# The first MLP's down projection: 14 of its 22 K blocks plain, the last 8 as a chunk of seven half-size products

## The chip, the cores and the metric

The kernel runs on one core of a Trainium2 chip. The metric is the device time of one execution in microseconds (us); lower is better. Inputs and outputs are float32. A product of two float32 matrices is made of three TensorE matmuls on rounded parts: each operand is split into a high part (rounded to fp32r) and a low part (the operand less its high part), and high by high, high by low and low by high are summed.

## The reference

Two blocks of two layers with an MLP each, on a sequence of 512 tokens and a model width of 1024. The change is in the first layer's MLP, whose hidden width is 2816 (22 blocks of 128):

```python
h2 = rms_norm(x, ffn_norm)
u = causal_dwconv(h2 @ w_up, conv_w, conv_b)
a, bval = jnp.split(u, 2, axis=-1)
return x + (jax.nn.silu(a) * bval) @ w_down
```

After it comes a block with dilated window attention (its QKV projection is the next large product), an MLP of width 4096 (MLP2 of layer 0), a differential attention, and a second MLP of width 4096 (MLP2 of layer 1). In these:

```python
def sq_relu_mlp(xn, w_in, w_out):
    h = jax.nn.relu(xn @ w_in)
    return (h * h) @ w_out
```

## The kernel before

Activations are kept transposed: 128 features on the partitions, 512 tokens along the free axis. `x` is 8 such blocks of 128x512. Weights come from HBM in tiles of 128x1024 (512 KB) by SyncE's queue (SP) into the two halves of `stage`. ScalarE (ACT) writes the high part of a tile (`split_hi`, here `down_split_hi`), GpSimd (POOL) the low part (`split_lo`, here `down_split_lo`, in four instructions of 128x256), and a stage half is free for the next load when POOL is done with it (`lo_ready`). VectorE (DVE) reads the finished PSUM banks. Nothing orders the engines but semaphores, and each engine works its own instructions strictly in the order written in its block.

**The up projection of the first MLP** ends with `Q_UP` = 17 rounds of seven half-size products each (84 matmuls of 128x256 a round, L1309, L1310, L1317). Beside it, DVE and ACT do the convolution (L2065, L2924, L2927), the silu (L2071), and POOL forms block f of the gated hidden layer `f1[f]` (`f_made_of`, L760). A block f is needed in two parts: `f_high(f)` on ACT (L2135) and `f_low(f)` on DVE (L3024).

**The down projection** (`for d in range(KD)`, L1342 to L1376) makes the 8 output blocks d one after the other, each over all 22 blocks f: 22 x 3 matmuls of 128x512 into PSUM bank `G[d % 2]` (L1360 high by high, L1362 and L1339 high by low, L1369 low by high). Its 176 weight blocks are packed 8 to a tile, so `N_DOWN1` = 22 tiles and an output block is 2.75 tiles. Output block 0 has its high by low products (`first_by_low`, L1339) put last, since those low parts are made latest. When a block is done DVE adds the bank to `x[:, d]` (L3090) and forms the next layer's low input with `low_x` (L2591), and ACT its high part (L2242) and square (L2243). The bank may be written again for block d + 2 once DVE's addition has counted up `evac`.

**The seven half-size products** (Winograd's form of Strassen's algorithm) are used by MLP2's down projection: a chunk of 8 K blocks by 512 tokens is multiplied with 4 groups ("quads") of 256 output features. One quad is 7 products over 4 pairs of K blocks, 3 matmuls of 128x256 for each pair (`product`, L1735, L1736, L1744), 84 matmuls in place of 2 x 8 x 3 = 48 of 128x512. Its operands are sums of quarters: on the weights' side 8 highs by ACT (`quad_copy`, `quad_high`), 4 sums and 2 lows by DVE (`quad_sum`, `quad_low`), 5 lows by POOL (`quad_lows`); on the activations' side per pair of K blocks the four sums and seven high and low factors (`fc_hi`, `fc_lo`), made by ACT and DVE as the K blocks get ready. The seven results are added to `x` by DVE in quarters (`add_product`, L3512).

Of the kernel before, what the change touches and what calls it, by code (L numbers as in the profile page):

```python
# [16 lines left out]
F32 = mybir.dt.float32  # L17
F32R = mybir.dt.float32r
ALU = mybir.AluOpType
# [37 lines left out]
N_DOWN1 = KD * NF1 // KD  # L57
# [15 lines left out]
EVAC_SKIP = (N_UP1 + N_DOWN1) // 2 - KD // 2 - WO_HALVES  # L73
# [15 lines left out]
Q_LAST = 2 * N_CH * QUADS - 1  # L89
# [27 lines left out]
N_EARLY = 8  # L117
EARLY_AT = 4
POOL_LOWS = []
DVE_LOWS = [f for f in range(NF1) if f not in POOL_LOWS]  # L120
FFH_PREP = FF_PREP = 2 * QUADS
X_LOWS = QUADS + 1
FFH_BEFORE, FF_BEFORE = FFH_PREP + NF1, FF_PREP + len(DVE_LOWS)
# [7 lines left out]
def quad_at(l, n):  # L131

    return QUADS * (N_CH * l + n)


def fc_at(l, n, i):

    return N_FC * l + 2 * KD * n + 4 * i
# [37 lines left out]
def program(nc, x_in, params, consts, buckets, swa_table, weights, pairs, tables, out):  # L176
    with ExitStack() as ctx:
# [77 lines left out]
        f_home = [arena[:, N_IN_ARENA + 4 * c + b] for c in F_FREE for b in range(4)]  # L255
        f1_hi = [(w_hi, w_lo)[f // 2 % 2][:, f // 4].rearrange("p (a k) c -> p a (k c)", a=2)[:, f % 2] for f in range(N_EARLY)]
        f1_hi += f_home[N_EARLY:NF1]
        f1_lo = [arena[:, f] for f in range(N_IN_ARENA)] + f_home[NF1:]

        def down_hi(t):  # L260

            if t == T_DOWN1 + 3:
                return v_split[:, 0].rearrange("p b t f -> p (b t) f")
            if t == T_DOWN1 + 2:
                return bias_slots[:, 0:2].rearrange("p a (c f) -> p (a c) f", f=P)
            a = N_IN_ARENA + 4 * F_FREE[t % 2]
            return arena[:, a:a + 2].rearrange("p a (c f) -> p (a c) f", f=P)

        def down_lo(t):

            if t == T_DOWN1 + 3:
                return v_split[:, 1].rearrange("p b t f -> p (b t) f")
            if t == T_DOWN1 + 2:
                return bias_slots[:, 2:4].rearrange("p a (c f) -> p (a c) f", f=P)
            a = N_IN_ARENA + 4 * F_FREE[t % 2] + 2
            return arena[:, a:a + 2].rearrange("p a (c f) -> p (a c) f", f=P)
# [96 lines left out]
        up_moved, down_done = sem("up_moved"), sem("down_done")  # L373
# [130 lines left out]
        def _(sp):  # L504
# [109 lines left out]
            loads(T_DOWN1, T_QKV[0])  # L614
            sp.wait_ge(tables_saved, 80)
            for l, core in enumerate((dil, dif)):
                T = T_QKV[l]
                if l == 1:
                    loads(T, T + 2)
                    sp.wait_ge(dil.maxed, 8 * PAIRS)  # L620
                for p in range(2):
                    bias_load(core, tables[l], p, p, None)
                loads(T + 2 * l, T + 8)
# [18 lines left out]
        def _(pool):  # L642
# [60 lines left out]

            def mlp2_splits(l):

                for n in range(N_CH):
# [11 lines left out]
                    ends = n == N_CH - 1  # L718
                    for j in range(1, QUADS):
                        quad_lows(q + j, (HI_A11,))  # L720
                        if ends and j > 1:
                            square_sum(4 + 2 * l, 2 * j - 4)
                        quad_lows(q + j, (HI_A12,))
                        if ends and j > 1:
                            square_sum(4 + 2 * l, 2 * j - 3)
                        quad_lows(q + j, (HI_S4, HI_S3, HI_A22))
                square_sum(4 + 2 * l, 4)
                square_sum(4 + 2 * l, 5)
# [33 lines left out]
            def f_low(f):  # L762

                pool.wait_ge(ffh_ready, FFH_PREP + f + 1)
                nc.gpsimd.tensor_tensor(f1_lo[f], f1[f], f1_hi[f].bitcast(F32), ALU.subtract).then_inc(factor_low, 1)

            def down_low(t):

                for k in range(0, KD, KD // 4):
# [4 lines left out]
            def down_split_lo(t):  # L774

                pool.wait_ge(hi_ready, t + 1)
                down_low(t)
# [32 lines left out]
            down_split_lo(T_DOWN1 + 2)  # L810
            for f in POOL_LOWS:
                f_low(f)
            pool.wait_ge(ff_ready, FF_PREP + 20)
            down_split_lo(T_DOWN1 + 3)
            with pool.Fori((T_DOWN1 + 4) // 2, T_QKV[0] // 2) as m:
                for p_ in range(2):
                    pool.wait_ge(hi_ready, 2 * m + p_ + 1)
                    pool.wait_ge(tile_done, 2 * m + p_ - 1)
                    down_low(T_DOWN1 + 4 + p_)
            split_los(T_QKV[0], T_MLP2[0])  # L820
# [47 lines left out]
        def _(pe):  # L868
# [466 lines left out]
            def first_by_low(s_, ks):  # L1335

                for k, f in ks:
                    pe.wait_ge(ff_ready, FF_PREP + f + 1)
                    mm = pe.matmul(G[0][:], down_hi(T_DOWN1 + s_)[:, k], f1_lo[f], start=False, stop=(f == NF1 - 1))  # L1339
                mm.then_inc(hi_free if ks[-1][0] == KD - 1 else down_done, 1)  # L1340

            for d in range(KD):  # L1342
                pieces = []
                for f in range(NF1):
                    s_, k = divmod(d * NF1 + f, KD)
                    if k == 0 or f == 0:
                        pieces.append((s_, []))
                    pieces[-1][1].append((k, f))
                if d < 2:
                    pe.wait_ge(conv_2, 2 * (NF1 - 1))  # L1350
                else:
                    pe.wait_ge(evac[d % 2], T_MLP1 // 2 + WO_HALVES + d // 2)
                for s_, ks in pieces:
                    t = T_DOWN1 + s_
                    ends = ks[-1][0] == KD - 1
                    pe.wait_ge(hi_ready, t + 1)
                    for k, f in ks:
                        if d == 0:
                            pe.wait_ge(ffh_ready, FFH_PREP + f + 1)
                        pe.matmul(G[d % 2][:], down_hi(t)[:, k], f1_hi[f], start=(f == 0), stop=False)  # L1360
                        if d:
                            mm = pe.matmul(G[d % 2][:], down_hi(t)[:, k], f1_lo[f], start=False, stop=False)  # L1362
                    if d and ends:
                        mm.then_inc(hi_free, 1)
                    if d == 0 and s_ == 2:
                        first_by_low(*pieces[0])
                    pe.wait_ge(lo_ready, t + 1)
                    for k, f in ks:
                        mm = pe.matmul(G[d % 2][:], down_lo(t)[:, k], f1_hi[f], start=False, stop=(d > 0 and f == NF1 - 1))  # L1369
                    if ends:  # L1370
                        mm.then_inc(tile_done, 1)
                    elif d and f == NF1 - 1:
                        mm.then_inc(down_done, 1)
                if d == 0:
                    for s_, ks in pieces[1:]:
                        first_by_low(s_, ks)  # L1376
# [7 lines left out]
            def layer_a():  # L1384
# [89 lines left out]
                norm(2)  # L1474
                tile(T // 2, 1, xn_hi, xn_lo)
# [237 lines left out]

            def product(l, n, q, k, quads):

                j, s = q % QUADS, q % 2
                region = R2 if k in (HI_A12, HI_A22) else R5 if k in (HI_S1, HI_S4) else R1[s][:, 0:HS]
                fresh = k in (HI_A11, HI_S1, HI_A12, HI_A22)
                f = FACTORS[k]
                if quads[0] == 0:  # L1720
                    pe.wait_ge(slot_high, UP_HIGHS + N_HIGH * q + k + 2)
                    read = N_PROD * q + {HI_A11: -N_PROD, HI_S1: -2, HI_A12: 0, HI_S2: 1, HI_S4: 2, HI_S3: 4, HI_A22: 3}[k]
                    if q == Q_LAST and k in (HI_S3, HI_A22):
                        read = N_PROD * q + LAST_ADDS["u2" if k == HI_S3 else "p2"]
                    if read > 0:
                        pe.wait_ge(product_added, UP_ADDED + read)
                high = {F_B11: 1, F_T1: 2, F_B21: 3, F_B22: 3, F_T3: 4, F_T2: 4, F_T4: 4}[f]
                for i in quads:
                    w = slot_hi[k][:, i * P:(i + 1) * P]
                    if j == 0 and i == QUADS - 1 and f == F_T2:  # L1730
                        pe.wait_ge(factor_low, X_LOWS + N_CH * l + n + 1)
                    elif j == 0:
                        pe.wait_ge(ffh_ready, FFH_BEFORE + fc_at(l, n, i) + high)
# [2069 lines left out]
```

## Time and profile before

| | us |
|---|---|
| median of 3 runs | 1696.07 |
| lowest and highest | 1695.65, 1696.42 |
| the profiled execution, its own time | 1695.82 |
| its span, first to last instruction | 1693.8 |
| TensorE busy in the span | 1684.6 (99%) |
| VectorE busy | 1128.9 (67%) |
| ScalarE busy | 909.3 (54%) |
| GpSimd busy | 1018.8 (60%) |

The profile is of one execution. A busy time is the union of an engine's instructions, and the duration of a matmul includes its pipelined end, so the pace of matmuls is read from the distance of their starts or from the chain of waits, not from the mean of one. The chain of waits lists what released what, back from the last instruction; a piece that stands in it with `x8` is eight instructions in a row. Stretches below are given in us from the start of the span: the down projection is 422.38 to 542.16, and the last chunk of MLP2 of layer 0 is 1060.72 to 1101.04.

### The profile page before, as it was taken

Reading aid. Unit: us, or ns where it says so; the run is one execution under the profiler, and the core shown is the slowest. Engines: PE = TensorE matmul, PEld = TensorE weight load, DVE = VectorE, ACT = ScalarE, POOL = GpSimd, SP = SyncE. Lnnn points to the kernel's source line nnn. Section 1 sums busy time; section 2 is a strip of 40 time slices with the busy share of each in tenths; the row PEclk is TensorE's granted clock in tenths of the full one; section 3 lists DMA queues with packets and bytes.
Section 4 is the critical chain, followed back from the end, with each engine's and each line's share of the span. In section 5 each row is a group of like instructions: output and inputs, shape, how many; then the busy total and the mean of one; then the engine's idle time right before and its main releaser. Section 6 shows DMA issues by size and latency. Waiting matters only on the chain.

```text
span 1693.8 us, 28396 instructions
## 1 busy us (share of the span) xinstructions
PE 1684.6 (99%) x10031; PEld 1460.3 (86%) x10031; DVE 1128.9 (67%) x2244; ACT 909.3 (54%) x1665; POOL 1018.8 (60%) x1071
## 2 busy tenths in 40 slices
PE   9999999999999999999999999999999999999998
PEld 7778889999888888888989898977777889898988
DVE  6875888887412455667766666777777675757576
ACT  5665658787423444345444444656565553535355
POOL 6543688777554444357575757755554666666666
PEclk9999999999999999999999999999999999999999
DMA  5221333222334322223323233232331343333332
GB/s 194 77 69 63 106 110 125 101 100 88 92 95 143 97 69 85 75 87 112 113 87 112 89 111 96 98 121 84 119 106 50 90 135 100 99 100 100 100 100 75
DMA packets 48555, 168.37 MB, mean 99 GB/s; under 512 B 5216, under 2 KB 6512, under 8 KB 48432
## 3 DMA queue, kind: packets, MB, share of 16 engines
q1 hardware_dynamic: 48144, 166.23, 30.5%
q8 instruction: 73, 1.20, 0.3%
q10 hardware_dynamic: 288, 0.53, 0.1%
q14 instruction: 50, 0.41, 0.1%
HBM read 164.49 MB, written 2.24 MB: 98 GB/s over the span
## 4 chain that ended last, share of the span: by engine, by line
PE 96%; DVE 2%; ACT 1%; POOL 1%; DMA 1%; issue 1%; DVEq 0%; ACTq 0%
PE bank L970 19%; PE bank L889 7%; PE bank L888 7%; PE bank L894 7%; PE bank L1735 6%; PE bank L1744 6%; PE bank L1736 6%; PE bank L1309 3%; PE bank L1317 3%; PE bank L1310 3%; PE bank L988 3%; PE bank L994 3%; PE bank L989 3%; PE bank L1369 2%; PE bank L1360 2%; PE bank L1362 2%
## 5 line engine op out<-in xcount | busy, mean ns | idle before, releaser
L648 POOL TENSOR_TENSOR w_lo<-stage,w_hi 128x256 fp32r<-128x256 f32 x648 | 512.5, 823 | 414.7 <-ACT w_hi L1797 212.8
L1797 ACT ACTIVATE w_hi<-stage 128x1024 fp32r<-128x1024 f32 x162 | 170.6, 1053 | 162.0 <-PE bank L970 49.7
L888 PE MATMUL bank<-xn_hi,w_hi 128*128 128x512 f32 x544 | 211.8, 389 | 0.0
L889 PE MATMUL bank<-xn_lo,w_hi 128*128 128x512 f32 x544 | 211.7, 389 | 0.0
L970 PE MATMUL bank<-xn_hi,w_hi 128*128 128x512 f32 x464 | 188.1, 405 | 0.0
L970 PE MATMUL bank<-xn_lo,w_hi 128*128 128x512 f32 x464 | 181.8, 392 | 0.0
L3512 DVE TENSOR_TENSOR x_space<-x_space,bank 128x256 f32<-128x256 f32 (+1 forms) x217 | 96.7, 454 | 86.9 <-PE bank L1744 85.0
L1744 PE MATMUL bank<-arena 128*128 128x256 f32 x896 | 146.6, 283 | 0.0
L894 PE MATMUL bank<-xn_hi,w_lo 128*128 128x512 f32 x544 | 135.0, 389 | 0.0
L1735 PE MATMUL bank<-arena 128*128 128x256 f32 x512 | 128.8, 283 | 0.0
L1736 PE MATMUL bank<-arena 128*128 128x256 f32 x512 | 128.7, 283 | 0.0
L1744 PEld LDWEIGHTS bank<-arena 128*128 128x128 f32 x896 | 124.8, 192 | 0.0
L970 PE MATMUL bank<-xn_hi,w_lo 128*128 128x512 f32 x464 | 123.5, 398 | 0.0
L894 PEld LDWEIGHTS bank<-xn_hi,w_lo 128*128 128x128 f32 x544 | 102.1, 188 | 21.2
L889 PEld LDWEIGHTS bank<-xn_lo,w_hi 128*128 128x128 f32 x544 | 102.1, 188 | 21.0
L888 PEld LDWEIGHTS bank<-xn_hi,w_hi 128*128 128x128 f32 x544 | 102.2, 188 | 21.0
L3532 DVE TENSOR_TENSOR arena<-tmp,arena 128x256 fp32r<-128x256 f32 (+2 forms) x120 | 107.7, 918 | 3.9 <-ACT arena L2536 2.5
L970 PEld LDWEIGHTS bank<-xn_hi,w_hi 128*128 128x128 f32 x464 | 87.2, 188 | 21.0 <-issue 4.2
L970 PEld LDWEIGHTS bank<-xn_hi,w_lo 128*128 128x128 f32 x464 | 84.7, 188 | 21.5 <-issue 4.7
L970 PEld LDWEIGHTS bank<-xn_lo,w_hi 128*128 128x128 f32 x464 | 87.3, 188 | 16.4
L1735 PEld LDWEIGHTS bank<-arena 128*128 128x128 f32 x512 | 98.3, 192 | 0.1
L1736 PEld LDWEIGHTS bank<-arena 128*128 128x128 f32 x512 | 98.3, 192 | 0.0
(517 smaller groups left out, 4352.3 us busy)
## 6 DMA issues: line engine op xcount, KB each, us to landing
stage<-weights SPq DMA_DIRECT2D x185, 512.0 KB, 3.5
stage<-pairs SPq DMA_DIRECT2D x48, 512.0 KB, 3.6
prob<-pairs SPq DMA_DIRECT2D x32, 512.0 KB, 3.6
bias<-table SPq DMA_DIRECT2D x11, 896.0 KB, 5.9
xn_raw<-pairs SPq DMA_DIRECT2D x16, 512.0 KB, 4.0
out<-y SPq DMA_DIRECT2D x8, 256.0 KB, 2.3
x_space<-x_in SPq DMA_DIRECT2D x3, 512.0 KB, 7.4
bias<-swa_table SPq DMA_DIRECT2D x4, 256.0 KB, 3.7
```

Source lines behind the costliest of these rows:

```text
L648: ins = nc.gpsimd.tensor_tensor(w_lo[:, p_, ks], stage[:, p_, ks], w_hi[:, p_, ks].bitcast(F32), ALU.subtract)
L888: pe.matmul(G[p_][:], w_hi[:, p_, k], hi[:, k], start=(first and k == ks[0]), stop=False)
L889: mm = pe.matmul(G[p_][:], w_hi[:, p_, k], lo[:, k], start=False, stop=False)
L894: mm = pe.matmul(G[p_][:], w_lo[:, p_, k], hi[:, k], start=False, stop=(last and k == ks[-1]))
L970: mm = pe.matmul(G[p_][:], (w_hi if i < 2 * KD else w_lo)[:, p_, k], (xn_lo if i < 2 * KD and i % 2 else xn_hi)[:, k], start=(i == 0), sto ...
L988: pe.matmul(G[dd][:], w, ff_hi[:, k], start=(k == k0), stop=False)
L1735: pe.matmul(region, w, fc_hi[:, i, f], start=(fresh and i == 0), stop=False, skip_group_check=True)
L1736: pe.matmul(region, w, fc_lo[:, i, f], start=False, stop=False, skip_group_check=True)
L1744: mm = pe.matmul(region, w, fc_hi[:, i, f], start=False, stop=(i == QUADS - 1), skip_group_check=True)
L1797: act.activation(w_hi[:, p_], stage[:, p_], ACT.Copy).then_inc(hi_ready, 1)
L3512: dve.tensor_tensor(dst, dst, src, ALU.add).then_inc(product_added, 1)
L3532: dve.tensor_tensor(fc_lo[:, i, a:b + 1].rearrange("p c s -> p (c s)"), src, fc_hi[:, i, a:b + 1].rearrange("p c s -> p (c s)").bitcast(F3 ...
```

## The change

- The 22 blocks of the down projection are split 6 + 8 + 8. The first 16 tiles (`N_DOWN1 = 2 * KD`) are one tile an output block: tiles 0 to 7 hold 6 K blocks each (the rest of the tile is padding, loaded as before), tiles 8 to 15 hold 8. `down_tile(j)` makes 18 or 24 matmuls in the order high by high and high by low in turn, then low by high; each of the 16 ends with an addition to `x` (`add_down`).
- The last 8 K blocks (`f1[14]` to `f1[21]`) are a chunk of seven half-size products, made by the functions of MLP2, which are taken out of `fast` and `mlp2` (`factor_half`, `first_sums`, `first_highs`, `chunk_highs`, `chunk_lows`, `chunk_adds`, `fast_down`). Their factors are made while tiles 8 to 15 are multiplied, without the relu and square that MLP2 has there. The first chunk's first two additions stand behind all factor work in place of inside it.
- `N_EARLY` (blocks whose high and low parts are made during the up projection) goes from 8 to 6. The parts of blocks 6 to 13 go to other homes, and each waits for the end of the up projection (`product_done`, `N_PROD * Q_UP`).
- The first QKV tiles are loaded when the chunk's last quad has left `stage`; the biases of the attention are loaded after the chunk's quads; the norm's two matmuls go from between the first two QKV tiles to inside the second.

```diff
-N_DOWN1 = KD * NF1 // KD
+NF_PLAIN = 14
+N_DOWN1 = 2 * KD
-N_EARLY = 8
+N_EARLY = 6
 ...
 SyncE
-            loads(T_DOWN1, T_QKV[0])
+            loads(T_DOWN1, T_DOWN1 + KD + 4)
+            sp.wait_ge(tile_done, T_DOWN1 + KD)
+            for r in range(2):
+                quad_load(0, r)
+            loads(T_DOWN1 + KD + 4, T_QKV[0])
+            for r in range(2):
+                sp.wait_ge(lo_ready, T_QKV[0] - 1 + r)
+                quad_load(1, r)
+            for j in range(2, QUADS):
+                for r in range(2):
+                    quad_load(j, r)
             sp.wait_ge(tables_saved, 80)
+            sp.wait_ge(tile_done, T_QKV[0])
+            for p in range(2):
+                bias_load(dil, tables[0], p, p, None)
+            sp.wait_ge(slot_low, UP_LOWS + 5 * QUADS)
             for l, core in enumerate((dil, dif)):
                 T = T_QKV[l]
+                loads(T, T + 2)
 ...
 GpSimd
-                for k in range(0, KD, KD // 4):
+                for k in range(0, KD if t >= T_DOWN1 + KD else N_EARLY, KD // 4):
 ...
+                if t >= T_DOWN1 + 2:
+                    pool.wait_ge(tile_done, t - 1)
 ...
 TensorE
+            def down_tile(j):
+
+                t, d = T_DOWN1 + j, j % KD
+                fs = list(range(N_EARLY) if j < KD else range(N_EARLY, NF_PLAIN))
+                if j < 2:
                     pe.wait_ge(conv_2, 2 * (NF1 - 1))
                 else:
+                    pe.wait_ge(evac[d % 2], T_MLP1 // 2 + WO_HALVES + j // 2)
+                pe.wait_ge(hi_ready, t + 1)
 ...
+            for j in range(N_DOWN1):
+                down_tile(j)
+            fast_down(-1, N_CH - 1)
 ...
                 tile(T // 2, 0, xn_hi, xn_lo, ready=(xn_ready, KD * 2, KD))
-                norm(2)
-                tile(T // 2, 1, xn_hi, xn_lo)
+                tile(T // 2, 1, xn_hi, xn_lo, inside=2)
 ...
 ScalarE
-                    act.wait_ge(product_done, N_PROD * (Q_UP - 1) + f // 4 + 1)
+                    act.wait_ge(product_done, N_PROD * Q_UP)
                 act.activation(f1_hi[f], f1[f], ACT.Copy).then_inc(ffh_ready, 1)
 ...
             silu(NF1 - 1)
-            f_high(14)
-            f_high(15)
+            for f in range(N_EARLY, NF_PLAIN - 2):
+                f_high(f)
             down_split_hi(T_DOWN1 + 2)
-            for f in range(16, NF1):
+            for f in range(NF_PLAIN - 2, NF_PLAIN):
                 f_high(f)
-            down_split_hi(T_DOWN1 + 3)
             load_exp_and_ln()
 ...
+            for t in range(T_DOWN1 + 3, T_DOWN1 + KD + 2):
+                down_split_hi(t)
+            act.wait_ge(f_made, NF1)
+            act.wait_ge(tile_done, T_DOWN1 + KD)
+            act.wait_ge(ff_ready, FF_BEFORE)
+            for e in range(KD):
+                factor_half(-1, N_CH - 1, e, f1[NF_PLAIN + e])
+                if e < KD - 2:
+                    down_split_hi(T_DOWN1 + KD + e + 2)
+                first_highs(0, e)
+            chunk_highs(-1, N_CH - 1)
+            for p_ in range(2):
+                split_hi(T_QKV[0] // 2, p_)
+            split_fast(-1, 0, 3)
 ...
 VectorE
             conv(NF1 - 1, 1)
-            for f in DVE_LOWS:
-                if f > 10:
-                    f_low(f)
+            for f in range(N_EARLY, NF_PLAIN):
+                f_low(f)
 ...
+            def add_down(j):
+
+                dve.wait_ge(tile_done, T_DOWN1 + j + 1)
+                dve.tensor_tensor(x[:, j % KD], x[:, j % KD], G[j % 2][:], ALU.add).then_inc(evac[j % 2], 1)
+
+            for j in range(KD):
+                add_down(j)
             dve.wait_ge(f_made, NF1)
-            dve.memset(acc, 0.0).then_inc(acc_zero, 1)
 ...
+            for e in range(KD):
+                i, p_ = e // 2, e % 2
+                if p_ == 0:
+                    dve.wait_ge(ff_ready, FF_BEFORE + fc_at(-1, N_CH - 1, i))
+                add_down(KD + e)
+                factor_half(-1, N_CH - 1, e, f1[NF_PLAIN + 2 * i], f1[NF_PLAIN + 2 * i + 1])
+                first_sums(0, e)
+            add_product(0, HI_A11)
+            add_product(0, HI_S1)
+            chunk_adds(-1, N_CH - 1)
```

How the change moves instructions shows best at three places. First VectorE where the up projection ends, before (L3024 is `f_low`, L2924 and L2927 the convolution, L3090 the first addition to `x`):

```order
L3009 TENSOR_TENSOR bank<-rstd,bank 128x256 [waits product_done,up_moved]
L3024 TENSOR_TENSOR arena<-arena_raw,arena 128x512 [waits ffh_ready]
L2924 SCALAR_TENSOR_TENSOR tmp<-bank,par,tmp 128x511 [waits conv_0]
L2927 SCALAR_TENSOR_TENSOR tmp<-bank,par,tmp 128x510 [waits conv_1]
L3016 TENSOR_TENSOR bank<-xn_raw,bank 128x256 [waits conv_2,up_moved]
L3017 TENSOR_TENSOR bank<-xn_raw 128x256
L3024 TENSOR_TENSOR arena<-arena_raw,arena 128x512 [waits ffh_ready] x2
L2924 SCALAR_TENSOR_TENSOR tmp<-bank,par,tmp 128x511 [waits conv_0]
L2927 SCALAR_TENSOR_TENSOR tmp<-bank,par,tmp 128x510 [waits conv_1]
L3024 TENSOR_TENSOR arena<-arena_raw,arena 128x512 [waits ffh_ready] x5
L3024 TENSOR_TENSOR arena<-xn_raw,arena 128x512 [waits product_done,ffh_ready] x6
L3090 TENSOR_TENSOR x_space<-x_space,bank 128x512 [waits down_done,acc_zero]
```

The same place on VectorE with the change (L2935 and L2938 are the convolution, L3035 `f_low`, L3242 `add_down`; the x8 and the single one are the additions of tiles 0 to 8):

```order
L2935 SCALAR_TENSOR_TENSOR tmp<-bank,par,tmp 128x511 [waits conv_0]
L2938 SCALAR_TENSOR_TENSOR tmp<-bank,par,tmp 128x510 [waits conv_1]
L3027 TENSOR_TENSOR bank<-xn_raw,bank 128x256 [waits conv_2,up_moved]
L3028 TENSOR_TENSOR bank<-xn_raw 128x256
L3035 TENSOR_TENSOR xn_hi<-arena_raw,bias_slots 128x512 [waits product_done,ffh_ready] x6
L3035 TENSOR_TENSOR xn_lo<-arena_raw,bias_slots 128x512 [waits product_done,ffh_ready]
L3035 TENSOR_TENSOR xn_lo<-arena_raw,rstd_slot 128x512 [waits product_done,ffh_ready]
L3242 TENSOR_TENSOR x_space<-x_space,bank 128x512 [waits tile_done] x8
```

Before, 14 `f_low` stood ahead of the first addition, three of them ahead of the last convolution; now 8 stand there, all behind it.

TensorE at the end of tile 1 and the start of tile 2 with the change (L1366 and L1369 are the high by high and high by low matmuls of `down_tile`, L1373 the low by high ones):

```order
L1373 MATMUL bank<-w_hi,arena 128x512 [waits lo_ready]
L1373 MATMUL bank<-w_hi,arena 128x512
L1373 MATMUL bank<-w_lo,arena 128x512 x2
L1373 MATMUL bank<-w_hi,arena 128x512 x2
L1366 MATMUL bank<-w_hi,arena 128x512 [waits hi_ready,evac0]
L1369 MATMUL bank<-arena 128x512
```

The wait on `evac0`, for the bank of the output block two before, now stands 36 matmuls after the start of the down projection; before it stood 132 matmuls after it.

VectorE where the chunk begins, with the change (L3165 to L3180 are `factor_half` of the last K block, L3134 is `add_product`):

```order
L3242 TENSOR_TENSOR x_space<-x_space,bank 128x512 [waits tile_done]
L3165 TENSOR_TENSOR tmp<-xn_raw 128x256
L3168 TENSOR_TENSOR tmp<-xn_raw,tmp 128x256
L3170 TENSOR_TENSOR tmp<-xn_raw,tmp 128x256 [waits u_ready]
L3154 TENSOR_TENSOR arena<-xn_raw,arena 128x512 [waits ffh_ready]
L3175 TENSOR_TENSOR arena<-tmp,arena 128x256 [waits factor_made]
L3180 TENSOR_TENSOR arena<-tmp,arena 128x2x256 [waits ffh_ready]
L3134 TENSOR_TENSOR x_space<-x_space,bank 128x256 [waits product_done] x2
```

In MLP2 the two L3134 stand after the first L3165 and after L3175; here both stand last.

## Rows read from the trace of the kernel before

**Rows 1.** The page: busy time by engine, and the chain of waits by engine.

```profile
PE 1684.6 (99%) x10031; PEld 1460.3 (86%) x10031; DVE 1128.9 (67%) x2244; ACT 909.3 (54%) x1665; POOL 1018.8 (60%) x1071
...
PE 96%; DVE 2%; ACT 1%; POOL 1%; DMA 1%; issue 1%; DVEq 0%; ACTq 0%
```

**Rows 2.** Waits of TensorE in the whole span: total us, times, longest.

```profile
PE bank L1154 <- DVE arena L2644: 1.5, 1, 1.5
```

**Rows 3.** Busy times of three stretches: length, PE, PEld, DVE, ACT, POOL, clock, DMA.

```profile
422.38:542.16 119.78, 119.78 (x530) 99.05 (x529) 29.88 (x40) 39.06 (x49) 64.77 (x87) 1.00 0.35 111
1060.72:1101.04 40.32, 40.32 (x338) 40.32 (x337) 31.15 (x61) 25.31 (x44) 29.98 (x24) 1.00 0.27 87
1017.21:1060.72 43.51, 43.51 (x194) 36.01 (x194) 29.62 (x40) 21.94 (x35) 29.98 (x33) 1.00 0.34 109
```

**Rows 4.** The chain of waits around 422 and 542: start, us, what.

```profile
421.90 0.48 PE bank L1317 x4
422.38 1.84 PE bank L1360 x8
...
542.16 0.23 PE bank L888
```

**Rows 5.** VectorE in order of time, 419 to 438: start, us, instruction, idle before.

```profile
419.95 1.25 DVE L3024 TENSOR_TENSOR arena<-arena_raw,arena 128x512 fp32r<-128x512 f32 x1
...
423.51 1.28 DVE L3024 TENSOR_TENSOR arena<-arena_raw,arena 128x512 fp32r<-128x512 f32 x2
...
425.49 0.75 DVE L2927 SCALAR_TENSOR_TENSOR tmp<-bank,par,tmp 128x510 f32<-128x510 f32 x1
426.16 5.83 DVE L3024 TENSOR_TENSOR arena<-arena_raw,arena 128x512 fp32r<-128x512 f32 x5
431.91 4.78 DVE L3024 TENSOR_TENSOR arena<-xn_raw,arena 128x512 fp32r<-128x512 f32 x6
...
437.55 0.69 DVE L3090 TENSOR_TENSOR x_space<-x_space,bank 128x512 f32<-128x512 f32 x1 [0.33 <-PE bank L1339]
```

**Rows 6.** ScalarE in order of time, 424 to 433.

```profile
424.83 1.14 ACT L2135 ACTIVATE arena<-arena_raw 128x512 fp32r<-128x512 f32 x2
425.88 1.05 ACT L2144 ACTIVATE bias_slots<-stage 128x1024 fp32r<-128x1024 f32 x1
426.83 3.22 ACT L2135 ACTIVATE arena<-xn_raw 128x512 fp32r<-128x512 f32 x6
...
431.01 1.28 ACT L1837 ACT_TABLE_LOAD   x1
```

**Rows 7.** GpSimd in order of time, 426 to 439.

```profile
426.39 1.61 POOL L760 TENSOR_TENSOR xn_raw<-tmp 128x512 f32<-128x512 f32 x1 [3.19 <-DVE tmp L2927]
427.95 4.62 POOL L771 TENSOR_TENSOR bias_slots<-stage,bias_slots 128x256 fp32r<-128x256 f32 x4
```

**Rows 8.** VectorE and ScalarE in MLP2's fourth factor step, 1039 to 1047.

```profile
1039.78 0.68 DVE L3542 SCALAR_TENSOR_TENSOR tmp<-bank,rstd 128x512 f32<-128x512 f32 x1
...
1041.13 0.62 ACT L2519 ACTIVATE tmp<-tmp 128x512 f32<-128x512 f32 x1
...
1044.12 0.85 ACT L2536 ACTIVATE arena<-tmp 128x768 fp32r<-128x768 f32 x1 [1.70 <-DVE tmp L3557]
...
1045.35 1.05 ACT L1797 ACTIVATE w_hi<-stage 128x1024 fp32r<-128x1024 f32 x1
```

**Rows 9.** VectorE in the same chunk's last factor step, 1061 to 1066.

```profile
1061.26 0.68 DVE L3542 SCALAR_TENSOR_TENSOR tmp<-bank,rstd 128x512 f32<-128x512 f32 x1
1062.64 0.42 DVE L3552 TENSOR_TENSOR tmp<-tmp 128x256 f32<-128x256 f32 x1 [0.70 <-ACT tmp L2519]
...
1065.37 0.68 DVE L3566 TENSOR_TENSOR arena<-tmp,arena 128x512 fp32r<-128x512 f32 x1
```

**Rows 10.** From that chunk into QKV of layer 1: ScalarE, then the chain.

```profile
1099.56 1.06 ACT L1797 ACTIVATE w_hi<-stage 128x1024 fp32r<-128x1024 f32 x1 [0.22 <-DMA stage<-weights]
...
1101.04 0.23 PE bank L888
```

**Rows 11.** The span's first matmuls: duration ns min/median/max, first and last start.

```profile
L1154 PE MATMUL bank<-arena x9: 537/628/792, 1.5 to 5.0; 128*128 128x512 f32 x9
```

More of the change, by code:

```diff
@@ L702, in square_sum, with chunk_lows @@
                 nc.gpsimd.tensor_tensor(acc, acc, tmp[:, d % 2], ALU.add).then_inc(acc_done, 1)
+            def chunk_lows(l, n):
+                q, ends = quad_at(l, n), n == N_CH - 1
+                for j in range(1, QUADS):
+                    quad_lows(q + j, (HI_A11,))
+                    if ends and j > 1:
+                        square_sum(4 + 2 * l, 2 * j - 4)
+                    quad_lows(q + j, (HI_A12,))
+                    if ends and j > 1:
+                        square_sum(4 + 2 * l, 2 * j - 3)
+                    quad_lows(q + j, (HI_S4, HI_S3, HI_A22))
+                if ends:
+                    square_sum(4 + 2 * l, 4)
+                    square_sum(4 + 2 * l, 5)
             def mlp2_splits(l):
@@ L717, in mlp2_splits @@
                     quad_lows(q, (HI_S3, HI_A22))
[L718 to L728, printed above, removed]
+                    chunk_lows(l, n)
                 if l == 0:
@@ new lines, in fast_down @@
+            def fast_down(l, n):
+                every, most, last = list(range(QUADS)), list(range(QUADS - 1)), [QUADS - 1]
+                for j in range(QUADS):
+                    q = quad_at(l, n) + j
+                    if q == Q_LAST:
+                        for k in LAST_ORDER[:-1]:
+                            product(l, n, q, k, every)
+                        last_means(0)
+                        product(l, n, q, HI_A22, every)
+                        last_means(1)
+                        return
+                    product(l, n, q, HI_A11, every)
+                    product(l, n, q, HI_S1, every)
+                    if j == 0:
+                        product(l, n, q, HI_A12, most)
+                        product(l, n, q, HI_S2, most)
+                        product(l, n, q, HI_A12, last)
+                        product(l, n, q, HI_S2, last)
+                    else:
+                        product(l, n, q, HI_A12, every)
+                        product(l, n, q, HI_S2, every)
+                    product(l, n, q, HI_S4, every)
+                    product(l, n, q, HI_S3, every)
+                    product(l, n, q, HI_A22, every)
@@ L3069, in _ @@
                 c_01(q)
-                if not more:
-                    f_low(N_EARLY)
-                elif EARLY_AT <= q < EARLY_AT + N_EARLY:
+                if EARLY_AT <= q < EARLY_AT + N_EARLY:
                     f_low(q - EARLY_AT)
@@ L3613, in fast @@
-                if ends and l == 0:
-                    for k in range(2):
-                        low_fast(l, QUADS - 1, k)
-                        last_square(4 + 2 * l, KD - 2 + k)
+                    factor_half(l, n, e, tmp[:, 0], tmp[:, 1], quad_at(l, n))
+                    first_sums(quad_at(l, n), e)
+                chunk_adds(l, n)
             def mlp2(l):
```

653 lines of the change are left out of this document (295 added, 358 removed).

## The prediction

> **What bounds the kernel now.** I read the page's busy times and chain first [rows 1]: TensorE is busy 99% of the span and holds 96% of the chain, so a saved matmul is saved time, and time that TensorE waits is lost in full. Then TensorE's waits [rows 2]: the longest in the whole span is 1.5 us, at its very start. Then the stretches [rows 3]: in the down projection and in a chunk of MLP2, TensorE is busy for the whole stretch at granted clock 1.00, while no other engine is above 77% of it. The chain at both ends of the down projection [rows 4] shows that TensorE goes from the last up product straight to L1360 at 422.38, and at 542.16 straight to the first QKV matmul. So nothing waits here before; the question is the number of matmuls, and whether the helpers still keep ahead.
>
> **What the matmuls are worth.** The down projection has 528 matmuls of 128x512; eight of them stand for 1.84 us in the chain [rows 4], and 119.78 / 528 = 0.2269 us each [rows 3]. A chunk of MLP2 has 336 matmuls of 128x256 in 40.32 us, 0.12 us each [rows 3]. Eight plain tiles of 24 matmuls took 43.51 us there [rows 3]. The change keeps 336 plain matmuls (14 x 8 x 3) and turns 192 into one chunk: 40.32 in place of 43.51, a gain of **3.2 us**. In columns the saving is one eighth (43.51 / 8 = 5.4 us); since a matmul of half the columns takes more than half the time, 2.2 us of it do not come.
>
> **The first additions, the dearest term.** Tiles 0 to 7 are now 18 matmuls, 4.08 us, each an output block of its own. Tile 2 needs bank `G[0]`, thus VectorE's addition of tile 0 (wait on `evac0`). It is due at 422.38 + 36 x 0.2267 = **430.54**. Before, block 2 came after 132 matmuls, 22 us later than that, and the addition at 437.55 [rows 5] was in good time. In VectorE's queue all eight `f_low(6..13)` stand ahead of it, and they can start only after the last convolution, which ended at 426.24 [rows 5]. The three `f_low` that stood ahead of that convolution are gone; as the convolution also waits for ScalarE I let it end only 0.3 us earlier, 425.95 (an estimate; at most it is 1.28 earlier, the length of two of them).
> One `f_low` took 0.64 us when GpSimd was idle (two in 1.28) and 1.17 us beside GpSimd (five in 5.83, while GpSimd was at work from 426.39 to 432.57) [rows 5, 7]. ScalarE makes six highs from 424.83 at 0.54 each (six in 3.22), then the high part of tile 2 (1.05), so at about 429.1, then the last two highs, ready at 430.1 [rows 6]. GpSimd works on `f1[21]` for 1.6 us from about 426.1, is idle until tile 2's high is there at 429.1, then makes that tile's low part (three instructions now, at 4.62 / 4 each: 3.5 us) and at once tile 3's [rows 7]. So VectorE does 0.2 + 1.4 lows until 427.7, 2.2 until 429.1, and the last 4.2 at 1.17, until about 433.95; the addition takes 0.69 [rows 5]: 434.65. TensorE waits **4.1 us** before tile 2. Bounds: if only ScalarE's last high held VectorE up, 430.1 + 0.64 + 0.69 = 431.4, a wait of 0.9; if all eight took 1.17, 425.95 + 9.4 + 0.7 = 436.0, a wait of 5.5. I take the middle because the rows of this very place show both prices. Behind this addition the one of tile 1 follows within 0.7 us, and no later tile finds its bank full: additions of 0.69 every 4.08 us.
>
> **The weights of tiles 2 to 9.** In 4.08 us ScalarE spends 1.05 [rows 6] and GpSimd three instructions of up to 1.16 us (3.5) [rows 7]. 0, as both are under the tile's time; the padding's load I take as free: a tile is loaded every 4.08 us where it was every 5.44, and DMA was busy 35% of the stretch [rows 3]. The exponential table load (1.28) [rows 6] is moved ahead of tile 3's high, due 438.8: hidden.
>
> **The factors, beside tiles 8 to 15.** ScalarE now has the high part of tile e + 2 behind step e's factors, and these wait for VectorE's addition of tile e. Odd steps are the long ones. In MLP2's, from the start of VectorE's bank read (1039.78) to the end of ScalarE's last factor copy (1044.97) went 5.2 us, of which 1.3 belong to the square that is left out here: 3.9, plus the tile's high 1.05 [rows 8], 4.9 us. A tile is 5.44. VectorE began 0.8 us late in that step, being busy with the quad sums (tile 3's end is 1017.21 + 4 x 5.44 = 1038.97) [rows 3, 8]; with that it is 5.7, 0.3 late, less what the missing square of the step before gives. I take **0.2 us** for all steps. Bounds: 0; and, if the steps were as slow as MLP2's with its square, 1.6 us in each of two steps, 3.2.
>
> **Start and end of the chunk.** TensorE reaches the fourth product, which needs the first product added, after 33 x 0.12 = 3.96 us. VectorE's additions stand behind all factor work now. In MLP2 the last step took from 1061.26 to 1066.05, 4.8 us [rows 9]; without the wait for the square (0.7) and the two additions (0.7), and with the first one at its end (0.4), 3.8: just in time. I take **0.1**, bounds 0 and 1.0 (three of the instructions slowed by GpSimd as above). Into QKV the order is that of MLP2's last chunk, where the second tile's high ended at 1100.62 and TensorE went on at 1101.04 without a gap [rows 10]: 0, with 1 us as the upper bound for the loads now issued that late. The two matmuls of the norm are only moved.
>
> **Sum.** -3.2 + 4.1 + 0.2 + 0.1 = +1.2 us on the profiled execution's 1695.82 gives 1697.0; the median of the runs lies 0.25 above that execution, so **1697.3**. That is +0.07%: within 0.2% (3.4 us, about what a measurement of this kernel can tell from no change). A saving of matmuls that is given back in one new wait.
>
> **Rivals.**
> - *The wait is short.* If VectorE's lows follow ScalarE's highs closely, the wait is the 0.9 us above, or even none, and with the other terms (0.3) the change is worth 2.0 us: 1694.1; with no wait anywhere 3.2: 1692.9. For it: an `f_low` at 0.64 would do eight in 5.1. Against: GpSimd is at work beside them for most of the time in exactly this place [rows 5, 7]. Chance 0.14.
> - *The wait lets TensorE's clock fall.* The only slow matmuls of the trace are the nine after the wait at the start: their starts are 0.44 us apart (8 distances in 3.5 us) [rows 11], twice the 0.227 of the same shape later, which is what 1.2 in place of 2.4 GHz would do. If the 4 us gap did it too, nine such matmuls more would cost 1.9 us: 1699.2; with the longest wait 1700.6. For it: no gap like it exists in the trace [rows 2], so nothing shows that the clock survives one; against: the matmuls around it are dense on both sides. The Trainium skill (TensorE: Matmul & The Clock Gate, Part 1) says that the array's clock is halved after an idle window and restored by sustained work; by that rule an idle gap like this one could bring it about. This is the page that speaks against the change; no row here shows it after the start. Chance 0.15.
> - *The weights come late (the slower side).* If ScalarE's new order (factors first, then the tile's high) misses the 5.44 us in two steps by MLP2's full price, TensorE waits 3.2 us there and not 0.2: 1700.3. It decides once an odd step takes over 5.44 from the end of its tile to the end of the next-but-one's high, and the whole change is slower by over 0.2% once all waits pass 6.6 us. For it: my own count has it 0.3 us from the edge [rows 8]. Against: the square is gone. Chance 0.13.
> The forecast itself keeps 0.58.
>
> **How the numbers follow.** The likeliest case gives 1697.3. The range starts at 1693.0, the case without the wait, and ends at 1700.5, where the third rival and most of the second lie. Faster by over 0.2% (under 1692.7) needs every wait to be hidden and something more: 0.04. Slower by over 0.2% (over 1699.5): the third rival, the second with a wait over 4.1, and the longest waits of the forecast: 0.20. The rest, 0.76, is no change.
>
> **What would show it.** In the profile after, 336 matmuls of `down_tile` at 0.227 and 336 of `product` at 0.12 right behind them; TensorE waiting some 4 us for VectorE's first `x` addition at 430.5, the largest wait in the list; VectorE's eight `f_low` in a row of about 8 us right ahead of it; TensorE from 422.38 to the first QKV matmul about 121 us long in place of 119.78. The clock rival would show as matmul starts 0.44 apart after the gap; the third as waits on ScalarE's tile highs before tiles 13 and 15. Wrong I am if TensorE has no wait before tile 2, or one over 5.5 us, or if it waits after the chunk.

## The result, and the profile after

| | before | after |
|---|---|---|
| median of the runs | 1696.13 us (20 runs) | 1699.38 us (20 runs) |
| lowest to highest | 1695.65 to 1696.63 | 1698.70 to 1700.69 |
| profiled execution: time, span | 1695.82, 1693.8 | 1699.65, 1697.8 |
| mean granted clock of TensorE | 0.999 | 0.998 |

The changed kernel takes 3.25 us more, a ratio of 1.002 with a 95% interval of 1.0014 to 1.0026. That is 2.1 us above the forecast of 1697.3, and 1.1 us inside its upper end. The runs of after are also spread over 2.0 us, those of before over 1.0. Both facts turn out to have one main cause.

The page of after, busy time by engine and the chain of waits by engine; they answer to [rows 1]:

```profile
PE 1683.7 (99%) x10175; PEld 1465.6 (86%) x10175; DVE 1172.5 (69%) x2323; ACT 924.5 (54%) x1700; POOL 1032.5 (61%) x1065
...
PE 93%; DVE 2%; POOL 2%; issue 1%; ACT 1%; DMA 1%; DVEq 0%; SPq 0%; ACTq 0%; POOLq 0%
```

TensorE is busy 0.9 us less than before with 144 instructions more: the matmuls were saved, but not all of their time. Its share of the chain fell from 96% to 93%. TensorE's waits in the whole span (line, releaser: us in total, times, longest), which answer to [rows 2]:

```profile
PE bank L1366 <- DVE x_space L3242: 4.1, 1, 4.1
PE bank L1173 <- DVE arena L2655: 1.5, 1, 1.5
...
PE bank L969 <- DVE arena L2794: 0.4, 1, 0.4
```

L1366 is the first matmul of a plain down tile and L3242 VectorE's addition of a tile to `x`. This is the forecast wait, before tile 2 and of the forecast size. L969 is the norm's matmul in QKV, and new. The stretches of after (length, PE, PEld, DVE, ACT, POOL, granted clock, DMA share, GB/s), which answer to [rows 3]:

```profile
422.58:434.89 12.31, 8.19 (x36) 6.42 (x36) 11.01 (x15) 9.14 (x14) 7.08 (x7) 1.00 0.24 64
434.89:438.56 3.67, 3.67 (x9) 2.96 (x10) 0.54 (x1) 0.00 (x0) 0.62 (x1) 0.54 0.68 208
438.56:504.23 65.67, 65.67 (x290) 54.19 (x290) 30.20 (x46) 23.89 (x35) 37.91 (x49) 1.00 0.34 107
504.23:544.60 40.37, 40.37 (x335) 40.23 (x334) 30.54 (x59) 22.24 (x39) 29.13 (x22) 1.00 0.38 135
```

Tiles 0 and 1 and the wait are the first row. The last row holds nearly all of the chunk, but begins half a microsecond before it; from its own first matmul (504.69) to QKV's first (545.11) the chunk takes 40.42 us, so MLP2's 40.32 again. The second row is what the forecast did not contain: right behind the wait the granted clock is 0.54. In the chain, in order of time (start, us, what), the same place reads:

```profile
434.24 0.61 DVE x_space L3242
434.85 0.04 issue
434.89 0.79 PE bank L1366
435.68 0.43 PE bank L1369
436.11 0.43 PE bank L1366
436.54 0.43 PE bank L1369
...
438.24 0.32 PE bank L1369
438.56 0.23 PE bank L1366
```

Eight matmuls of 128x512 follow each other at 0.43 us (the first is 0.79, with its own latency, and the eighth 0.32), and from 438.56 on at 0.23. That is 1.2 GHz and then 2.4 GHz. At 0.227 each the eight would have taken 1.8 us of these 3.67, so 1.9 us more were lost: about 0.3 to the first matmul's latency after any wait (it takes 0.50 even at full clock, see the filled gap below) and 1.6 to the clock. The ledger of this execution, whose span is 4.0 us longer: matmuls -3.2, wait +4.1, clock and restart +1.9, the down projection's start +0.2 (422.58 for 422.38), the later tiles and the chunk +0.1 together, and +0.9 us at the start of QKV, where the chain reads:

```profile
539.40 5.58 DMA stage<-weights
...
545.00 1.06 ACT w_hi L1798
...
551.71 1.16 DVE arena L2794
552.87 0.04 issue
552.91 0.50 PE bank L969
```

QKV's first two weight tiles landed late (the DMA piece is the second one's), and what stands behind their high parts in ScalarE's queue reached the norm's matmul 0.4 us late; the low products of the first tile were a little late too.

The cause of the wait is VectorE's queue (start, us, instruction, instructions), answering to [rows 5]:

```profile
425.43 0.75 DVE L2938 SCALAR_TENSOR_TENSOR tmp<-bank,par,tmp 128x510 f32<-128x510 f32 x1
426.10 5.87 DVE L3035 TENSOR_TENSOR xn_hi<-arena_raw,bias_slots 128x512 fp32r<-128x512 f32 x6
431.89 1.22 DVE L3035 TENSOR_TENSOR xn_lo<-arena_raw,bias_slots 128x512 fp32r<-128x512 f32 x1
433.03 1.20 DVE L3035 TENSOR_TENSOR xn_lo<-arena_raw,rstd_slot 128x512 fp32r<-128x512 f32 x1
434.16 1.27 DVE L3242 TENSOR_TENSOR x_space<-x_space,bank 128x512 f32<-128x512 f32 x2
```

L3035 is `f_low`. Eight of them take from 426.10 to 434.2, and the two additions stand behind. GpSimd in the same stretch, answering to [rows 7]:

```profile
426.33 1.61 POOL L779 TENSOR_TENSOR xn_raw<-tmp 128x512 f32<-128x512 f32 x1 [4.78 <-DVE tmp L2938]
429.28 6.22 POOL L785 TENSOR_TENSOR arena<-stage,arena 128x256 fp32r<-128x256 f32 x6 [1.34 <-ACT arena L2145]
```

### The profile page after: what moved, and what is told of

The parts are those of the page before. It is cut to its first block, busy times and chain, and to the rows that moved or that the text cites. A ratio compares the mean times of both kernels' runs of the same rounds, so it can differ in the third digit from the quotient of the medians.

```text
span 1697.8 us, 28831 instructions
## 1 busy us (share of the span) xinstructions
PE 1683.7 (99%) x10175; PEld 1465.6 (86%) x10175; DVE 1172.5 (69%) x2323; ACT 924.5 (54%) x1700; POOL 1032.5 (61%) x1065
## 4 chain that ended last, share of the span: by engine, by line
PE 93%; DVE 2%; POOL 2%; issue 1%; ACT 1%; DMA 1%; DVEq 0%; SPq 0%; ACTq 0%; POOLq 0%
PE bank L989 19%; PE bank L913 7%; PE bank L908 7%; PE bank L907 7%; PE bank L1397 6%; PE bank L1406 6%; PE bank L1398 6%; PE bank L1328 3%; PE bank L1336 3%; PE bank L1329 3%; PE bank L1007 3%; PE bank L1013 3%; PE bank L1008 3%; PE bank L1654 1%; PE bank L1366 1%; PE bank L1369 1%
## 5 line engine op out<-in xcount | busy, mean ns | idle before, releaser
L3134 DVE TENSOR_TENSOR x_space<-x_space,bank 128x256 f32<-128x256 f32 (+1 forms) x245 | 109.4, 455 | 95.9 <-PE bank L1406 94.0
L1406 PE MATMUL bank<-arena 128*128 128x256 f32 x1008 | 165.0, 283 | 0.0
L1397 PE MATMUL bank<-arena 128*128 128x256 f32 x576 | 145.0, 283 | 0.0
L1398 PE MATMUL bank<-arena 128*128 128x256 f32 x576 | 144.8, 283 | 0.0
L1406 PEld LDWEIGHTS bank<-arena 128*128 128x128 f32 x1008 | 140.4, 192 | 0.0
L913 PEld LDWEIGHTS bank<-xn_hi,w_lo 128*128 128x128 f32 x544 | 102.0, 188 | 21.3 <-POOL w_lo L662 0.2
L908 PEld LDWEIGHTS bank<-xn_lo,w_hi 128*128 128x128 f32 x544 | 102.2, 188 | 21.0
L3154 DVE TENSOR_TENSOR arena<-tmp,arena 128x256 fp32r<-128x256 f32 (+2 forms) x127 | 114.5, 921 | 5.0 <-ACT arena L2295 3.4
L1397 PEld LDWEIGHTS bank<-arena 128*128 128x128 f32 x576 | 110.6, 192 | 0.2
L1398 PEld LDWEIGHTS bank<-arena 128*128 128x128 f32 x576 | 110.6, 192 | 0.0
L1397 PE MATMUL bank<-arena,v_split 128*128 128x256 f32 x432 | 108.8, 283 | 0.0
L1398 PE MATMUL bank<-arena,v_split 128*128 128x256 f32 x432 | 108.8, 283 | 0.0
```

Of the source, the lines that this page charges most:

```text
L908: mm = pe.matmul(G[p_][:], w_hi[:, p_, k], lo[:, k], start=False, stop=False)
L913: mm = pe.matmul(G[p_][:], w_lo[:, p_, k], hi[:, k], start=False, stop=(last and k == ks[-1]))
L1397: pe.matmul(region, w, fc_hi[:, i, f], start=(fresh and i == 0), stop=False, skip_group_check=True)
L1398: pe.matmul(region, w, fc_lo[:, i, f], start=False, stop=False, skip_group_check=True)
L1406: mm = pe.matmul(region, w, fc_hi[:, i, f], start=False, stop=(i == QUADS - 1), skip_group_check=True)
L3134: dve.tensor_tensor(dst, dst, src, ALU.add).then_inc(product_added, 1)
```

## The experiments

Three things were open. Is the wait all that the change gives back, or does it cost more than its length? Is it the clock that makes it cost more? And why do the eight `f_low` take 8.1 us? Theory A: the time after is that of a kernel without the wait (1692.9), plus the wait, plus a clock cost that the wait brings about. Rival B: the wait costs its length alone, and the remaining 2 us come from elsewhere (the weights' transfers into the factors or into QKV). The edits are against the changed kernel.

**Two `f_low` ahead of the additions.** Six of the eight operations stand behind the first two additions. No work is added or left out.

```
-            for f in range(N_EARLY, NF_PLAIN):
+            for f in range(N_EARLY, N_EARLY + 2):
                 f_low(f)
...
-            for j in range(KD):
+            add_down(0)
+            add_down(1)
+            for f in range(N_EARLY + 2, NF_PLAIN):
+                f_low(f)
+            for j in range(2, KD):
                 add_down(j)
```

> The changed kernel with one thing moved: two of VectorE's eight low parts stay ahead of the additions of tiles 0 and 1, the other six follow them. Theory (one bank wait of 4.1 us, a TensorE clock that falls in it and costs 1.7 us, 0.9 us at the chunk's end): both of the first go, span 5.8 us under the changed kernel's 1697.8, time about 1693.6, under the kernel before. Rival (the helpers are late as a whole, this wait only comes first): the wait turns up again before tile 4 or 8 and the time falls by 2 us or less, to 1697 or more.

Measured: 1692.88 us (1692.65 to 1693.28, 11 runs) beside 1696.07 (33 runs), a ratio of 0.9982 with an interval of 0.9973 to 0.9991; span 1691.0. VectorE there:

```profile
425.96 2.39 DVE L3035 TENSOR_TENSOR xn_hi<-arena_raw,bias_slots 128x512 fp32r<-128x512 f32 x2
428.28 0.67 DVE L3242 TENSOR_TENSOR x_space<-x_space,bank 128x512 f32<-128x512 f32 x1
430.67 0.69 DVE L3242 TENSOR_TENSOR x_space<-x_space,bank 128x512 f32<-128x512 f32 x1 [1.72 <-PE bank L1373]
431.28 3.03 DVE L3035 TENSOR_TENSOR xn_hi<-arena_raw,bias_slots 128x512 fp32r<-128x512 f32 x4
```

The addition of tile 0 now starts at 428.28 and has VectorE free for it; TensorE's list of waits no longer has L1366. The whole stretch of down projection and chunk is one block of busy TensorE (same columns as the stretches above):

```profile
422.40:541.60 119.20, 119.20 (x685) 105.47 (x684) 74.05 (x123) 58.81 (x93) 78.34 (x82) 1.00 0.36 118
```

The window runs 2.5 us past the chunk's end (QKV's first matmul is at 539.09 in the chain), and TensorE is busy there too.

This version is 3.2 us faster than the kernel before (1696.07 - 1692.88) and 6.5 faster than the one after. So the saved matmuls are worth what was forecast, all that is lost hangs on this one wait, and nothing else of the change (factors, chunk, transfers) costs anything measurable. It is also 0.7 us faster than the 1693.6 expected, and the 0.9 us at QKV's start, which the expectation had left in, is absent from its trace as well. The place of six instructions in one queue decides the sign of the change.

**Six ahead.** The same edit with `N_EARLY + 6`, for a wait of middle length.

> Six of the eight low parts stay ahead of the additions of tiles 0 and 1. The wait before tile 2 should be about 1.9 us (the sixth ended at 431.97, the addition 0.6 later, tile 2 due at 430.8). If the clock falls only in a longer gap: about 1693.6 + 1.9 = 1695.5, matmuls after it at 0.227 us. If any gap brings it down: 1697.2, matmuls after it at 0.43 us.

Measured: 1696.68 us (1694.90 to 1697.05, 11 runs), ratio 1.0002 (0.9993 to 1.0011), with a wait of 1.9 us before tile 2. The chain behind it:

```profile
432.08 0.69 DVE x_space L3242
...
432.81 0.50 PE bank L1366
433.30 0.24 PE bank L1369
...
434.00 0.23 PE bank L1366
434.23 0.42 PE bank L1369
...
436.79 0.43 PE bank L1369
437.21 1.58 PE bank L1373 x6
438.80 0.23 PE bank L1366
```

Behind this shorter wait TensorE goes on at full clock for five matmuls, and only at 434.23, 1.4 us after it is at work again, do starts fall to 0.43 apart, until within the six low products at 437.21. So the clock can fall some matmuls after the wait is over. The median is not the time without a wait plus the wait, 1692.9 + 1.9 = 1694.8: only the lowest run (1694.90) is there, and the median lies 1.9 above it. The expectation's either-or did not happen; the runs show both cases, two of the 11 with a mean granted clock of 0.999 (1694.90 and 1695.27) and nine with 0.998 (1696.53 to 1697.05).

**Seven ahead.** `N_EARLY + 7`.

> Seven of the eight low parts stay ahead. The wait should be about 3.0 us. If the clock stays: about 1696.7; if it falls: 1698.4. Between this and six ahead and the changed kernel's eight it should show from what wait on the clock is lost.

Measured: 1697.80 us (1695.96 to 1699.13, 11 runs), ratio 1.0009 (1.0000 to 1.0018), with a wait of 3.0. The lowest run is again 1692.9 + 3.0 = 1695.9; the median is 1.9 above it. In the traced execution (1698.05) clock and fall are as in the run before: four matmuls at full clock, then eight slower. Three of the 11 runs have a mean granted clock of 0.999 (1695.96 to 1696.52), the others 0.998 or 0.997 (1697.55 and more).

**The gap filled.** TensorE does 16 matmuls of 128x512 into a bank that nobody reads, between tiles 1 and 2. The wait for VectorE stays; only the idling goes.

```
                 t, d = T_DOWN1 + j, j % KD
...
+                if j == 2:
+                    pe.wait_ge(product_added, 4 * Q_UP)
+                    for i in range(16):
+                        pe.matmul(TR[0][:], f1_hi[0][:, 0:P], f1_hi[i % N_EARLY], start=(i == 0), stop=(i == 15))
```

> The changed kernel with all eight low parts ahead, and 16 matmuls of 128x512 into an unused bank put between tiles 1 and 2 (their result is not used), which fill 3.6 of the 4.1 us. Theory (the slow matmuls after the wait are the fallen clock): VectorE's addition still comes at 434.9, but the matmuls of tile 2 run at 0.227 us each; 1.7 us less than the changed kernel, about 1697.7. Rival (they are slow for another reason, reads that collide with the load or the splits then under way): 1699.4, starts still 0.43 us apart.

Measured: 1697.12 us (1697.04 to 1697.38, 11 runs), ratio 1.0007 (0.9998 to 1.0016). The chain at the same place:

```profile
434.14 0.61 DVE x_space L3246
...
434.80 0.50 PE bank L1366
435.30 0.24 PE bank L1369
435.53 0.23 PE bank L1366
```

and tile 2's 12 high products (same columns as the stretches above):

```profile
434.80:437.81 3.01, 3.01 (x13) 2.52 (x14) 0.54 (x1) 0.00 (x0) 0.62 (x1) 1.00 0.49 167
```

Tile 2 starts at 434.80, where it started at 434.89 in the changed kernel: nothing of the useful work was moved. But every matmul behind it is 0.23 apart, and the kernel is 2.3 us faster than after (1699.38 - 1697.12) with more work in it. This is the direct proof of the clock's part, and its size: 1697.12 = 1692.88 + 4.2. The expectation's rival, reads that collide with the load or the splits then under way, is out: the DMA share is 0.49 in this stretch and the matmuls are at full pace. The filled gap also explains most of the spread, since with the clock kept up the 11 runs lie within 0.34 us, in place of 2.0.

**The changed kernel again**, for a second trace of it.

> The changed kernel once more, unaltered, for a second profile of it. Same wait before tile 2 (4.1 us) in each execution; the number of matmuls at 0.43 us after it should differ, and with it the time (1698.7 to 1700.7 in the runs so far). The first QKV tile's weights landed 4.7 us after their issue in the first profile and 3.9 in the kernel with two low parts ahead: if that is chance, it will differ here; if it belongs to the changed kernel, it is 4.7 again and TensorE again waits 0.4 us at the norm.

Measured: 1699.17 us (1698.74 to 1700.35, 10 runs), ratio 1.0019 (1.0010 to 1.0028), the profiled one 1699.98 with a span of 1698.1. The wait is 4.1 again. Tile 2's 12 high products in this execution (same columns as the stretches above):

```profile
434.75:440.23 5.48, 5.48 (x13) 4.32 (x14) 0.54 (x1) 0.00 (x0) 0.61 (x1) 0.50 0.44 147
```

5.48 us where 12 x 0.227 = 2.7 would do, and 0.2 more in the low products behind: 3.0 us to restart and clock (0.3 and 2.7), where the first trace had 1.9. The late weights at QKV's start are absent: the chain there goes through TensorE's matmuls without a gap. So the 0.9 us in the first ledger come in some executions and not in others, and the part that is in every execution is wait and clock.

**GpSimd quiet beside the eight operations.** GpSimd starts on tile 2's low part only after VectorE's addition of tile 0.

```
                 pool.wait_ge(hi_ready, t + 1)
+                if t == T_DOWN1 + 2:
+                    pool.wait_ge(evac[0], T_MLP1 // 2 + WO_HALVES + 1)
```

> All eight low parts stay ahead of the first addition, but GpSimd starts the low part of tile 2 only after that addition, so it is idle beside the last six of VectorE's low parts. Theory (each low part takes 1.2 us because GpSimd works beside it, 0.6 alone): the last low part ends with ScalarE's last high, near 430.9, the addition at 431.6, a wait of about 0.9 us in place of 4.1, time 1693.8 to 1695.7 with what the clock takes. Rival (they are slow for their operands' places): wait 4 us, time as the changed kernel's.

Measured: 1695.56 us (1694.87 to 1697.18, 11 runs), ratio 1.0001 (0.9992 to 1.0010), with a wait of 2.0 us; 0.9 was expected. VectorE:

```profile
425.91 4.80 DVE L3037 TENSOR_TENSOR xn_hi<-arena_raw,bias_slots 128x512 fp32r<-128x512 f32 x6
430.64 0.68 DVE L3037 TENSOR_TENSOR xn_lo<-arena_raw,bias_slots 128x512 fp32r<-128x512 f32 x1
431.24 0.68 DVE L3037 TENSOR_TENSOR xn_lo<-arena_raw,rstd_slot 128x512 fp32r<-128x512 f32 x1
431.84 1.27 DVE L3244 TENSOR_TENSOR x_space<-x_space,bank 128x512 f32<-128x512 f32 x2
```

Tile 2's 12 high products in this execution (1694.87):

```profile
432.57:435.59 3.02, 3.02 (x13) 2.52 (x14) 0.54 (x1) 0.00 (x0) 2.90 (x5) 1.00 0.00 0
```

Here a wait of 2.0 us passed without any fall of the clock, where the traced execution of six ahead lost it behind 1.9. The same kernel does both: six of these 11 runs have a mean granted clock of 0.999 (up to 1695.56) and five 0.998 (from 1696.33).

An `f_low` that took 1.22 us beside GpSimd takes 0.68 (0.60 from start to start) without it, and the eight end 2.3 us sooner. GpSimd therefore makes about 2.1 us of the wait. The other 2.0 stay because the first operations are still slow beside GpSimd's `f1[21]` (426.14 to 427.76 here), and because the eight take 5.9 us in all even so (425.91 to 431.84). The Trainium skill (GPSIMD Engine Reference, section 1, Specifications) says that GpSimd's SBUF interfaces are shared with VectorE, with contention where a VectorE instruction has two SBUF inputs. The rows agree: `f_low` reads two SBUF tensors and doubles, while the addition of tile 0, with one input in PSUM, took 0.61 us in the chain both beside GpSimd's work (L3242 of after, at 434.24) and with GpSimd idle (L3244 here, at 431.92).

**Ten ahead.** Two further operations of the kind behind the eight, for a longer wait.

```
+            for k in (2, 3):
+                dve.tensor_tensor(xn_lo[:, k], f1[NF_PLAIN - 1], f1_hi[NF_PLAIN - 1].bitcast(F32), ALU.subtract)
```

> Two further operations of a low part's size (their results are not used) stand behind the eight, ahead of the first addition. Wait before tile 2 about 6.4 us. If the clock's cost is the same once it has fallen: 1692.9 + 6.4 + 1.7 to 3.7 = 1701.0 to 1703.0, all runs over 1701; if it grows with the wait, more.

Measured: 1702.34 us (1701.34 to 1702.85, 5 runs), ratio 1.0036 (1.0022 to 1.0049), with a wait of 6.4 us; the chain behind it:

```profile
436.33 0.61 DVE x_space L3244
...
436.99 0.80 PE bank L1366
437.78 0.43 PE bank L1369
...
442.48 1.64 PE bank L1373 x6
```

2.3 us more wait than in the changed kernel cost 3.0 us more time (1702.34 - 1699.38). The clock's part hardly grew: here as in the second trace of the changed kernel it is the 12 high products and one or two of the low ones that run at half clock.

All together. The last column is the run's time less 1692.9 and less the wait of the profiled execution, for the lowest and the highest run; it holds the clock, the restart and whatever else that execution lost, such as the late weights at QKV's start. The kernel before took 1696.07 beside the first four versions and 1695.92 beside "GpSimd quiet" and "ten", so 0.1 or 0.2 us in a row mean nothing.

| version | wait | lowest, median, highest | cost beyond the wait |
|---|---|---|---|
| two ahead | 0 | 1692.65, 1692.88, 1693.28 | 0 |
| six ahead | 1.9 | 1694.90, 1696.68, 1697.05 | 0.1 to 2.3 |
| GpSimd quiet | 2.0 | 1694.87, 1695.56, 1697.18 | 0 to 2.3 |
| seven ahead | 3.0 | 1695.96, 1697.80, 1699.13 | 0.1 to 3.2 |
| eight (after) | 4.1 | 1698.70, 1699.38, 1700.69 | 1.7 to 3.7 |
| gap filled | 4.1 (tile 2's; TensorE is at work in it) | 1697.04, 1697.12, 1697.38 | 0.0 to 0.4 |
| ten | 6.4 | 1701.34, 1702.34, 1702.85 | 2.0 to 3.6 |

Theory A holds through all rows. B is out as the account of the 2 us: it has none for the filled gap; the late weights at QKV's start are all that is left of it, 0.9 us in one execution and nothing in another of the same kernel. Only one execution of each version was traced (two of the changed kernel), but the mean granted clock of TensorE, rounded to three digits, is on record for every run; 0.001 of it is 1.7 us of this span. It is 0.999 in all runs of "two ahead" and "gap filled". Over the whole table no run with 0.999 lies more than 0.7 us above 1692.9 plus its wait, and no run with 0.998 or less lies under 1.4. Within the changed kernel the 11 runs up to 1699.65 have 0.998, the nine from 1699.83 on 0.997 or 0.996. So the wide rows are wide because of the clock in the main. What decides in which executions a short wait brings it down is open.

## Why the prediction was right, and where it was off

The range and the sense (no gain, within 0.2% of the time before) were right; the central value was 2.1 us too low. The range held because its upper end had been drawn to take in most of the clock rival; the sum did not contain that term. Step by step:

- *The matmuls, -3.2.* Right: the version without a wait is 3.2 us faster than the kernel before.
- *The wait before tile 2, 4.1.* Right, in place, cause and size: 4.1 in the trace. The addition ended at 434.85 (434.65 forecast), since ScalarE, VectorE and GpSimd did in that place what [rows 5 to 7] had shown. The two prices of `f_low` (0.64 and 1.17) were the right ones: 0.60 to 0.68 alone and 1.2 beside GpSimd.
- *Weights of tiles 2 to 9, 0; table load, 0.* Right: TensorE has no wait there, and the load lies at 430.27, ahead of tile 3's high part.
- *Factors beside tiles 8 to 15, 0.2.* It was 0: the high part of tile 13 started at 486.44 and that of tile 15 at 497.95, and TensorE never waited for one. The margin was small, as the count had said: the high part of tile 15 ended at 498.99, about 0.4 us before that tile began. The same holds for the third rival (0.13), which did not occur.
- *The chunk's start, 0.1.* Right within its bounds: the fourth product started at 508.68, 0.07 us late.
- *The chunk's end, 0 with 1 as the upper bound.* One trace shows 0.9, the other 0. The first of QKV's two weight tiles took, from SyncE's issue to the start of ScalarE's high part, 4.74, 4.55 and 4.41 us where the norm's matmul waited for 0.4, 0.4 and 0.2 us (after, ten ahead, seven ahead), and 4.11, 3.98, 3.95, 3.93 and 3.70 in the other traces, where it did not. Why the landing varies is open.
- *The clock, a rival at 0.15 and 1.9 us.* This is the step that failed. The forecast said that the matmuls around the gap are dense on both sides and so left the clock's fall out of the sum. Its size was well estimated from [rows 11] (1.9; the filled gap says 2.3 at the median), its chance was not: with a 4.1 us wait every run of the changed kernel lies at least 1.3 us above the slowest run of the filled gap. The forecast's own row at the span's start already had the price, and with it in the sum the figure would have been 1699.2, against 1699.38 measured. What the forecast took for dense work on both sides did not protect the clock; in nine of 11 runs it did not even behind a wait of 1.9 us.

The Trainium skill (TensorE: Matmul & The Clock Gate, Part 1), which the prediction named as speaking against the change, says that the array's clock is halved after idling and comes back with sustained work. The rows agree: granted clock 0.54 behind the wait and 1.00 from 438.56 on. They add that the cost begins with waits shorter than the changed kernel's, in some executions and not in others.

## What to carry to other kernels

A wait of TensorE in a dense kernel has two prices, its length and the matmuls at 1.2 GHz behind it; here 4.1 us cost 6.5. Put the second into the sum wherever an edit opens a gap of the sizes seen here (1.9 to 6.4 us), and read the clock column behind the wait before looking for another cause. When a change makes the first output block complete sooner, look up what stands in front of its evacuation in the evacuating engine's queue: what was harmless while the first bank was asked for again after 132 matmuls (30 us) was all of the loss when that came after 36 (8 us), and moving six instructions behind two others was worth 6.5 us.

## What was not expected of the hardware

- TensorE's clock fell behind waits of 1.9 and 3.0 us, and there not at once: five and four matmuls went at full clock first. Behind a wait of 2.0 us in another trace it did not fall at all. The cost beyond one and the same wait differs from execution to execution, 0.1 to 2.3 us behind 1.9 and 1.7 to 3.7 behind 4.1, and this is in the main what made the runs of the changed kernel spread over 2.0 us, in place of 0.34 with the gap filled.
- 16 useless matmuls in a gap made the kernel 2.3 us faster.
- The issue-to-use time of the same weight tile's transfer lay between 3.7 and 4.7 us in eight traces of nearly the same program.
